# Weight slabs of four k-tiles in four buffers, and a later reload of x, in a one-core recurrent decoder trunk

## The reference

```python
for l in range(DEPTH):                                  # 2 layers
    mod = cs @ w_ada[l] + b_ada[l]                      # shifts, scales and gates from c
    h = rmsnorm(x, norm_mix[l]) * (1 + sc_m) + sh_m
    proj = h @ w_in[l]                                  # q/k/v, gates, merge gates
    o_a, o_b, o_c = gated_delta(proj), retention(proj), hgrn2(proj)   # chunked recurrences
    branch = einsum('blnv,nvd->blnd', [o_a, o_b, o_c], w_branch[l])
    merged = sum(sigmoid(proj_merge) * branch, axis=n)
    x = x + gt_m * (merged @ w_out[l])
    h = rmsnorm(x, norm_ffn[l]) * (1 + sc_f) + sh_f
    g, u = split(h @ w_gate_up[l])
    x = x + gt_f * ((silu(g) * u) @ w_down[l])
y = rmsnorm(x, final_norm)
```

## Time and profile before

| | |
|---|---|
| median of 3 runs | 2861.84 us (2857.17 to 2862.52) |
| profiled execution | 2855.05 us; its span from first to last instruction 2853.3 us |
| TensorE matmuls busy | 2567.6 us, 90% of the span |
| TensorE weight loads busy | 2443.5 us, 86% |
| VectorE busy | 1224.0 us, 43% |
| GpSimd busy | 1402.6 us, 49% |
| ScalarE busy | 442.8 us, 16% |
| mean granted TensorE clock | 0.946 |
| read from and written to memory | 239.65 MB, 21.17 MB; 91 GB/s over the span |

### The profile page before, as it was taken

The page is one execution under the profiler, slowest core; times in us unless marked ns, Lnnn a source line. Parts: engine busy times, 40 slices in busy tenths (PEclk is TensorE's granted clock), DMA queues, the critical chain, the costliest instruction groups (busy, mean ns, idle before and its releaser), DMA issues. The chain is left out here.

```text
span 2853.3 us, 47939 instructions
## 1 busy us (share of the span) xinstructions
PE 2567.6 (90%) x20358; PEld 2443.5 (86%) x20358; DVE 1224.0 (43%) x1537; ACT 442.8 (16%) x824; POOL 1402.6 (49%) x728
## 2 busy tenths in 40 slices
PE   4988899889988889999779798998999887999996
PEld 3878898889978889999758798888899787999996
DVE  4664513251742853233147634231427438332332
ACT  2421122020120010000024221310211210000001
POOL 1431234456445657776524322344554464677773
PEclk8998999999998989999979898999999998999998
DMA  8720113123223312222286101132241142223222
GB/s 303 254 66 23 30 38 115 49 74 107 80 64 109 93 60 85 86 90 81 63 315 210 40 23 30 44 105 71 70 127 49 60 128 67 77 83 93 89 79 72
DMA packets 126318, 264.01 MB, mean 93 GB/s; under 512 B 9617, under 2 KB 68497, under 8 KB 124305
## 3 DMA queue, kind: packets, MB, share of 16 engines
q1 hardware_dynamic: 126096, 260.86, 29.3%
HBM read 239.65 MB, written 21.17 MB: 91 GB/s over the span
## 5 line engine op out<-in xcount | busy, mean ns | idle before, releaser
L668 PE MATMUL gemm_psum<-h_hi_lo,w_hi_lo 128*128 128x272 f32 x12000 | 1638.3, 296 | 75.5 <-DVE h_hi_lo L1203 46.7
L668 PEld LDWEIGHTS gemm_psum<-h_hi_lo,w_hi_lo 128*128 128x128 f32 x12000 | 1566.1, 194 | 127.5 <-issue 90.5
L641 POOL TENSOR_TENSOR w_hi_lo<-w_raw,consts 128x1024 fp32r<-128x1024 f32 (+3 forms) x362 | 616.8, 1704 | 1385.7 <-PE gemm_psum L668 1250.1
L643 POOL TENSOR_TENSOR w_hi_lo<-w_raw,w_hi_lo 128x1024 fp32r<-128x1024 f32 (+3 forms) x362 | 786.6, 2173 | 28.4
L1833 ACT ACTIVATE tiles<-gemm_psum 128x544 f32<-128x544 f32 (+1 forms) x188 | 116.4, 624 | 1208.1 <-PE gemm_psum L668 1207.8
L668 PE MATMUL gemm_psum<-ffn_hi_lo,w_hi_lo 128*128 128x272 f32 x2112 | 266.5, 288 | 0.0
L668 PEld LDWEIGHTS gemm_psum<-ffn_hi_lo,w_hi_lo 128*128 128x128 f32 x2112 | 266.1, 188 | 0.0
L668 PE MATMUL gemm_psum<-o_hi_lo,w_hi_lo 128*128 128x272 f32 x1152 | 159.4, 294 | 18.4 <-POOL w_hi_lo L643 18.4
L1816 DVE TENSOR_TENSOR tiles<-gemm_psum,tiles 128x544 f32<-128x544 f32 x44 | 31.9, 725 | 319.4 <-PE gemm_psum L668 319.4
L668 PEld LDWEIGHTS gemm_psum<-o_hi_lo,w_hi_lo 128*128 128x128 f32 x1152 | 150.8, 192 | 20.2 <-POOL w_hi_lo L643 19.9
L1833 ACT ACTIVATE scratch<-mix_psum 128x512 f32<-128x512 f32 (+3 forms) x112 | 59.2, 547 | 410.1 <-PE mix_psum L947 196.6
(11 more groups left out here) (233 smaller groups left out, 2110.4 us busy)
## 6 DMA issues: line engine op xcount, KB each, us to landing
w_raw<-in_w_gu SPq DMA_DIRECT2D x88, 512.0 KB, 3.5
tiles<-in_w_ada SPq DMA_DIRECT2D x64, 512.0 KB, 4.9
w_raw<-in_w_merge SPq DMA_DIRECT2D x48, 384.0 KB, 3.0
w_raw<-in_w_first SPq DMA_DIRECT2D x34, 512.0 KB, 3.7
w_raw<-in_w_ret SPq DMA_DIRECT2D x32, 512.0 KB, 3.5
w_raw<-in_w_hg SPq DMA_DIRECT2D x32, 512.0 KB, 3.6
w_raw<-in_w_merge SPq DMA_DIRECT2D x48, 256.0 KB, 2.7
w_raw<-in_w_dn SPq DMA_DIRECT2D x32, 384.0 KB, 3.1
```

The costliest lines, as they stand in the source:

```text
L641: pool.tensor_tensor(hi, src, ones[:, 0:1].broadcast_to([P, words]), ALU.mult).then_inc(hi_done, 1)
L643: pool.tensor_tensor(lo, src, hi.bitcast(F32), ALU.subtract).then_inc(split_done, 1)
L668: mm = pe.matmul(GP[:, 2 * (tile % 2) + h, 0:HALF], whl[:, n % 2, a, j * P:(j + 1) * P], rhs[:, b, step, h * HALF:(h + 1) * HALF], start=s ...
```

## The change

A slab now has at most four k-tiles (512 words), and `raw` and `whl` have four buffers of that size instead of two of 1024 words; the memory is the same. A tile of 8 k-tiles becomes two slabs, a down tile of 11 three (4, 4 and 3), a branch tile stays one: 322 slabs a layer instead of 181. The waits look back four slabs instead of two. SP stays 8 slabs ahead of the stream instead of 4 (in the convolution stage: 6 beyond the tile's last slab), and loads 4 slabs at the start of a layer instead of 3. The second slab of a merge-gate tile is loaded in two pieces, since its weights lie in two places. The wait for the stored states and the reload of x stand behind 16 more k-tiles of the stream, which are the first four branch tiles of branch 2.

```diff
+SLOTS, SLOT_KT = 4, 4
...
-    def add(name, i, *parts):
+    def add(name, i, source, kt):
         mine = []
-        for source, kt in parts:
-            slabs.append((source, kt))
-            mine += [(len(slabs) - 1, j, kt) for j in range(kt)]
+        for first in range(0, kt, SLOT_KT):
+            n = min(SLOT_KT, kt - first)
+            slabs.append((source, first, n))
+            mine += [(len(slabs) - 1, j, n) for j in range(n)]
...
-            add(f"down{f}", i, ((f"dn_a{f}", i), 6), ((f"dn_b{f}", i), KF - 6))
+            add(f"down{f}", i, (f"dn{f}", i), KF)
...
-    raw = sb("w_raw", [P, 2, D])
-    whl = sb("w_hi_lo", [P, 2, 2, D], F32R)
+    raw = sb("w_raw", [P, SLOTS, SLOT_KT * P])
+    whl = sb("w_hi_lo", [P, SLOTS, 2, SLOT_KT * P], F32R)
...
-                        if n >= 2:
-                            sp.wait_ge(split_done, n - 1)
+                        if n >= SLOTS:
+                            sp.wait_ge(split_done, n - SLOTS + 1)
...
-                        load_slabs(TILES[tile][2][step][0] + 4)
+                        load_slabs(TILES[tile][2][step][0] + 2 * SLOTS)
...
-                load_slabs(3)
+                load_slabs(SLOTS)
...
-                    load_slabs(n + 4)
+                    load_slabs(last_slab(n) + SLOTS + 2)
...
                 store_states(2)
+                fill(4 * H, BASE["out"])
                 sp.wait_ge(sig("stored_sample"), 16 * H * 3)
                 sp.dma_start(X[:, :, :], y_out[:, :, :]).then_inc(sig("x_back"), 16)
...
-                    if n >= 2:
-                        pool.wait_ge(slab_done, n - 1)
-                    pool.wait_ge(landed[n % 2], landed_by[n])
+                    if n >= SLOTS:
+                        pool.wait_ge(slab_done, n - SLOTS + 1)
+                    pool.wait_ge(landed[n % SLOTS], landed_by[n])
```

More of the change, by code:

```diff
@@ L162, in block @@
         for i in range(count):
-            add(name, i, ((table, first + i), KD))
+            add(name, i, (table, first + i), KD)
     block("rows", "first", 0, 1)
@@ L177, in stream @@
         for i in range(KD):
-            add(f"gate{n}", i, ((f"gate{n}", i), KD))
+            add(f"gate{n}", i, (f"gate{n}", i), KD)
             if n < 2:
-                add(f"branch{n}", i, ((f"branch{n}", i), H))
+                add(f"branch{n}", i, (f"branch{n}", i), H)
     for i in range(KD):
-        add("branch2", i, (("branch2", i), H))
+        add("branch2", i, ("branch2", i), H)
     block("out", "out", 0, KD)
@@ L185, in stream @@
         for i in range(KF):
-            add(f"silu{f}", i, ((f"gu{f}", 2 * i), KD))
-            add(f"up{f}", i, ((f"gu{f}", 2 * i + 1), KD))
+            add(f"silu{f}", i, (f"gu{f}", 2 * i), KD)
+            add(f"up{f}", i, (f"gu{f}", 2 * i + 1), KD)
         for i in range(KD):
-            add(f"down{f}", i, ((f"dn_a{f}", i), 6), ((f"dn_b{f}", i), KF - 6))
+            add(f"down{f}", i, (f"dn{f}", i), KF)
     return tiles, slabs
@@ L414, in load_parts @@
     def load_parts(l, n):
-        source, kt = SLABS[n]
-        name, i = source
+        (name, i), first, kt = SLABS[n]
+        a, b = first * P, (first + kt) * P
         if name in ("first", "ret", "hg", "out"):
-            return [({"first": w_first, "ret": w_ret, "hg": w_hg, "out": w_out}[name][l, i], 0)]
+            return [({"first": w_first, "ret": w_ret, "hg": w_hg, "out": w_out}[name][l, i][:, a:b], 0)]
         m = int(name[-1])
         if name.startswith("gate"):
-            return [(w_merge[l, m, i, 0], 0), (w_merge[l, m, i, 1][:, 0:2 * P], 6 * P)]
+            if first == 0:
+                return [(w_merge[l, m, i, 0][:, a:b], 0)]
+            return [(w_merge[l, m, i, 0][:, a:6 * P], 0), (w_merge[l, m, i, 1][:, 0:2 * P], 6 * P - a)]
         if name.startswith("branch"):
             return [(w_merge[l, m, i, 1][:, 2 * P:6 * P], 0)]
[L425 to L433, removed]
+        return [({"gu": w_gu, "dn": w_dn}[name[:2]][l, m, i][:, a:b], 0)]
+    landed = [sig(f"slab_landed_{i}") for i in range(SLOTS)]
+    landed_by, total = [], [0] * SLOTS
+    for n, ((name, _), first, _) in enumerate(SLABS):
+        total[n % SLOTS] += 32 if name.startswith("gate") and first else 16
+        landed_by.append(total[n % SLOTS])
     hi_done, split_done, slab_done = sig("weights_hi"), sig("weights_split"), sig("slab_done")
@@ L551, in load_slabs @@
                         at[0] += 1
-                        words = SLABS[n][1] * P
-                        if n >= 2:
-                            sp.wait_ge(split_done, n - 1)
+                        if n >= SLOTS:
+                            sp.wait_ge(split_done, n - SLOTS + 1)
                         for src, o in load_parts(l, n):
-                            sp.dma_start(raw[:, n % 2, o:o + src.shape[-1]], src).then_inc(landed[n % 2], 16)
+                            sp.dma_start(raw[:, n % SLOTS, o:o + src.shape[-1]], src).then_inc(landed[n % SLOTS], 16)
                 def fill(n, limit):
                     for tile, step in feed.take(n, limit):
-                        load_slabs(TILES[tile][2][step][0] + 4)
+                        load_slabs(TILES[tile][2][step][0] + 2 * SLOTS)
                 def drain(limit):
@@ L634, in _ @@
             def _(pool):
-                for n, (source, kt) in enumerate(SLABS):
+                for n, (_, _, kt) in enumerate(SLABS):
                     words = kt * P
-                    if n >= 2:
-                        pool.wait_ge(slab_done, n - 1)
-                    pool.wait_ge(landed[n % 2], landed_by[n])
-                    src, hi, lo = raw[:, n % 2, 0:words], whl[:, n % 2, 0, 0:words], whl[:, n % 2, 1, 0:words]
+                    if n >= SLOTS:
+                        pool.wait_ge(slab_done, n - SLOTS + 1)
+                    pool.wait_ge(landed[n % SLOTS], landed_by[n])
+                    src, hi, lo = raw[:, n % SLOTS, 0:words], whl[:, n % SLOTS, 0, 0:words], whl[:, n % SLOTS, 1, 0:words]
                     pool.tensor_tensor(hi, src, ones[:, 0:1].broadcast_to([P, words]), ALU.mult).then_inc(hi_done, 1)
@@ L667, in k_tile @@
                         for h in range(2):
-                            mm = pe.matmul(GP[:, 2 * (tile % 2) + h, 0:HALF], whl[:, n % 2, a, j * P:(j + 1) * P],
+                            mm = pe.matmul(GP[:, 2 * (tile % 2) + h, 0:HALF], whl[:, n % SLOTS, a, j * P:(j + 1) * P],
                                            rhs[:, b, step, h * HALF:(h + 1) * HALF],
```

## The result

The changed kernel takes 2749.8 us (median of 4 runs, 2748.24 to 2752.72); the kernel before, on the same chip, 2860.32 (4 runs, 2857.17 to 2862.52). The ratio is 0.9619, 95% interval 0.9608 to 0.9631: 110 us faster, where 54 were forecast. The direction was right and the size was not.

A forecast was written before the change was run, and what follows sets the result against it. TensorE's work plus its idle stretches were taken as the bound, with 47.0 us of waits for GpSimd. Terms 24.6 + 22 + 10 - 1 - 2 = 53.6 us gave 2808 us, range 2785 to 2837.

The forecast's parts named there:

- the waits for GpSimd: TensorE's 47.0 us of waits for GpSimd's low part go near zero; the small ones, 18 waits, gain 24.6 us.
- the term of branch 2: Branch 2 of the merge, behind the reload of x: 11 us a layer gained, 22 in all, bounds 16 and 32.
- GpSimd becomes the bound: Rival, chance 0.09: pieces cost 3.23 us against 3.03 of matmuls in pure-stream tiles, 67 us lost, about 2876 us.
- The loads bind: Rival, chance 0.07: small weight loads or the reload hold up weights, the branch-2 gain goes, 2830 us.
- The price of 3.96 us a tile: Branch 2: a GpSimd piece of 2.50 us plus two wholly excluded VectorE instructions of 0.73, instead of 3.03.
- the move was given the credit: Branch 2: issued later, the reload of x is covered by 24 us of TensorE work and costs nothing.
- Shorter GpSimd instructions: VectorE steps of the recurrences wait for shorter GpSimd instructions: 10 us gained, bounds a loss of 4, a gain of 17.
- the pattern that was priced: Rotary step: L1237 waits 0.4 us for GpSimd instead of 2.2, four times 1.8, plus two small waits, 2.5 us.
- The chains gain more: Rival, chance 0.10: shorter instructions help every VectorE step beside GpSimd, busier TensorE keeps its high clock; gain 80, 2782 us.
- the output projection: Output projection: VectorE ends a little later beside GpSimd, -2 us, bounds -4 and +2.
- the layer start: Layer start: four pieces split at once instead of two slabs, 10.0 against 8.7 us; -1 in all, bounds -3 and +1.

The follow-up runs named there:

- experiment 5: The changed kernel with GpSimd splitting each slab in pieces of 256 words, four instructions a slab instead of two: 2751.66 us, ratio 0.9634.
- experiment 6: The changed kernel with two buffers of 512 words instead of four, SP 4 slabs ahead instead of 8: 2826.98 us, ratio 0.9891.
- experiment 2: The kernel before with only the later reload of x added: 2844.62 us, ratio 0.995.
- experiment 1: The changed kernel with the reload of x back at its old place, behind the store of the states: 2752.85 us, ratio 0.9636.
- experiment 4: The changed kernel with GpSimd splitting two neighbouring slabs of a tile by one pair of 1024-word instructions: 2800.83 us, ratio 0.9801.
- experiment 8: The changed kernel with GpSimd resting after two slabs until VectorE has made three of eight parts of h: 2753.41 us, ratio 0.9636.

## Why the prediction was wrong

**Right: the waits for GpSimd.** They were 47.0 us, 24.6 of them small and 22.4 inside the term of branch 2, and are gone; branch 2 has no idle time, GpSimd is at 1544.7 us (near 1600 forecast), L942 waits 6.6 (7 forecast). "GpSimd becomes the bound" is refuted by experiment 5, where GpSimd spends 268 us more without a wait of PE. "The loads bind" is refuted in this ring: 256 KB still land in 2.6 us, and of GpSimd's waits for weights only those for the convolution's are left (128.4 us), and no wait of PE ends on GpSimd. It is right for two buffers (experiment 6). The Trainium skill, "DMA: Bandwidth & Descriptors", section "Measured (HBM→SBUF, 128 partitions, SWDGE, issued from GpSimd)", advises transfers of 1 MiB and more. Here loads were cut to 256 and 128 KB and cost nothing that can be seen, since PE waits for none of them. The row of after, as in the earlier trace rows:

```profile
w_raw<-in_w_merge SPq DMA_DIRECT2D x96, 256.0 KB, 2.6
```

**Right in place, off in size: branch 2.** The term was 22 us; from the first matmul of the stage to the first output tile 38.6 became 23.9 us in layer 0 and 37.9 became 24.0 in layer 1, 28.6 together, inside the bounds of 16 and 32. Two of its steps were off. The price of 3.96 us a tile took VectorE's two instructions as wholly exclusive of GpSimd's; the round is 3.25 us, and GpSimd's lead hides the excess. The Trainium skill, "SBUF — State Buffer", section "SBUF: two separate sides", has an exclusive lock for a whole instruction. The trace agrees that the loser waits for the end (L1790, 0.58 us after GpSimd's), but a round of GpSimd alone is some 2.5 us, so two instructions of 0.73 add about 0.75 to it, half of the 1.46 that the strict reading adds. And the move was given the credit: alone it brings 14 us (experiment 2), with four buffers 3 or nothing (experiment 1). The depth of the ring does it. With long instructions the ring and the move bring 58 us (experiment 4), against the 46.6 of these two terms.

**Wrong: "Shorter GpSimd instructions", put at 10 us.** This is the step that failed. Experiment 4 gives it 51 us in the new ring: 36.8 of idle time and 15.1 of matmuls at a lower clock. Of that, the pattern that was priced, the rotary step ahead of L940, came out as priced: its waits fell from 16.9 us before, and 16.0 in experiment 4, to 6.6. What failed is the step from this pattern to the whole: the term was bounded by half of two lines of waits, 17 us. Other VectorE steps on the way to a matmul are held by GpSimd too: with long instructions back, the delta-rule stages lose 24.2 us (in layer 1 the inverse's own wait is 2.9 of the 14.2) and one output projection 5.2. The page shows the holding as VectorE's busy time, 1224.0 to 1055.9 us for the same 1537 instructions. A bound for the term had to come from there. It would have been a loose one: experiment 5 takes another 77 us off it and gains nothing. "The chains gain more" named this mechanism with a tenth of the chance, and its 80 us was short too.

**Missing: the clock.** The matmuls take 30.9 us less, about half by the ring (2567.6 to 2551.8 in experiment 4) and half by the shorter instructions. That this is the clock can be reckoned from the traces' clock records: matmuls were busy for 208.3 us at the lower level (1.2 GHz) before and for 148.1 after. Half of the difference, 30.1 us, is what they would save at the upper level (2.4 GHz), an estimate that takes a matmul at the lower level as twice as long; 24 matmuls at it took 5.81 us in experiment 2, the 24 of the merge above 3.15. Only the 120 matmuls of the earlier trace rows had been seen that way. Why the clock is granted more often is not shown. Over the whole span it goes with less idle time, but not stage by stage: in the delta-rule stage of layer 0 PE is idle for 10.1 us less and the clock falls from 0.89 to 0.87.

**Wrong in sign, small: the output projection and the layer start.** The output projection was put at -2 us; the stage takes 69.9 and 69.8 us instead of 71.9, as VectorE is held less there too. The layer start was put at -1, and the first matmul of layer 0 did come 0.4 us later (61.5 to 61.9). But VectorE's part of it, from its instruction on `mod` to that matmul, became shorter, 9.5 to 7.4 us in layer 0 and 8.1 to 7.4 in layer 1. What came later in layer 0 is the small matmuls ahead of it at the lower clock (experiment 8).

The two halves need each other: the depth with long instructions gives 58 us, short instructions in the old ring 0, both 110. So the 51 us hold in the new ring alone, and a sum of terms measured one by one would have missed half of the gain.

## What to carry to other kernels

Where GpSimd and VectorE work from SBUF side by side, look at the length of GpSimd's single instruction, not at its total: in the new ring, cutting it from 1.9 and 2.4 us to 1.1 and 1.4 was worth 51 us although GpSimd's total rose by 129 (1415.8 to 1544.7), and cutting it again was worth nothing that the runs could tell. The sign to look for is one line whose duration varies between its own minimum and a GpSimd instruction's. Then look whether a matmul waits behind that line: only such holding costs time. Buy the short pieces with depth, or the ring's waits take the gain back. And when much idle time of TensorE goes, look at the matmuls' own time too: here 30.9 us of the gain were matmuls at a higher clock.

## What was not expected of the hardware

Two VectorE instructions of 0.73 us lengthen a GpSimd round of 2.5 us to 3.25, not to 3.96. GpSimd's cost is not proportional to words: in experiment 5 a piece of 256 words takes 0.66 and 0.79 us, one of 512 in the changed kernel 1.07 and 1.36:

```profile
L648 POOL TENSOR_TENSOR w_hi_lo<-w_raw,w_hi_lo 128x256 fp32r<-128x256 f32 x1256 | 990.1, 788 | 98.4
L645 POOL TENSOR_TENSOR w_hi_lo<-w_raw,consts 128x256 fp32r<-128x256 f32 x1256 | 830.4, 661 | 795.9 <-PE gemm_psum L674 673.1 <-DMA w_raw<-in_w_first 118.0
```

```profile
L645 POOL TENSOR_TENSOR w_hi_lo<-w_raw,w_hi_lo 128x512 fp32r<-128x512 f32 x612 | 829.2, 1355 | 47.9
L643 POOL TENSOR_TENSOR w_hi_lo<-w_raw,consts 128x512 fp32r<-128x512 f32 x612 | 657.5, 1074 | 1093.4 <-PE gemm_psum L670 964.9 <-DMA w_raw<-in_w_first 128.4
```
